# The opening of a mixture-of-experts layer: routing from unnormed residuals, one turn to tokens, and a gather that holds the tokens

## The reference, cut to what matters

```python
h2 = rms_norm(x, norm2_g[l]) * (1.0 + scale2) + shift2
x = x + gate2 * expert_choice_ffn(h2, w_router[l], b_router[l], w_gate[l], w_up[l], w_down[l])

def expert_choice_ffn(h, w_router, b_router, w_gate, w_up, w_down):
    cap = (EC_CAPACITY_FACTOR * S) // N_EXPERTS            # 2 * 512 / 16 = 64 places per expert
    affinity = jax.nn.softmax(h @ w_router + b_router, axis=-1)
    gates, idx = lax.top_k(affinity.transpose(0, 2, 1), cap)
    xin = h[bidx, idx]                                      # 16 experts x 64 tokens x 1024
    hid = silu(xin @ w_gate) * (xin @ w_up)                 # 1024 -> 2048
    y = hid @ w_down * gates[..., None]                     # 2048 -> 1024
    return zeros_like(h).at[bidx, idx].add(y)
```

## Time and profile before

| | us |
|---|---|
| median of 3 runs | 2590.87 (2590.12 to 2594.27) |
| the profiled execution: its time | 2594.25 |
| the profiled execution: its span | 2592.4 |
| PE busy | 2382.4 (92%) |
| DVE, ACT busy | 1006.2 (39%), 620.6 (24%) |
| read from HBM | 590.37 MB |

### The profile page before, as it was taken

How to read it: one execution, slowest core, us unless ns; L and a number is a source line. 1 busy time by engine, 2 the same in 40 slices (tenths; PEclk the granted TensorE clock), 3 DMA queues, 4 the chain that set the end, 5 groups by cost and what they waited for, 6 DMA issues and landing times.

```text
span 2592.4 us, 23747 instructions
## 1 busy us (share of the span) xinstructions
PE 2382.4 (92%) x9961; PEld 1394.2 (54%) x9961; DVE 1006.2 (39%) x1616; ACT 620.6 (24%) x1002; POOL 112.4 (4%) x120
## 2 busy tenths in 40 slices
PE   5999988899999999999789979799898989989888
PEld 2445544588888788888667737333232323233222
DVE  4555463366663666564556372301111011101011
ACT  2112163333223333233446464110000000000000
POOL 2000000000000000000221312000000000000000
PEclk8999988999999999999899999899999999999999
DMA  9312330355553145550211203599999999999997
GB/s 352 105 65 81 109 118 0 114 182 190 174 184 128 49 163 195 195 179 33 89 49 33 94 29 130 215 427 429 431 430 432 430 431 431 431 430 432 429 431 316
DMA packets 121024, 594.04 MB, mean 229 GB/s; under 512 B 9346, under 2 KB 10880, under 8 KB 95318
## 3 DMA queue, kind: packets, MB, share of 16 engines
q1 hardware_dynamic: 117522, 583.23, 56.7%
q0 software_dynamic: 3088, 9.17, 1.0%
q10 hardware_dynamic: 308, 0.13, 0.0%
HBM read 590.37 MB, written 2.13 MB: 229 GB/s over the span
## 4 chain that ended last, share of the span: by engine, by line
PE 77%; DMA 12%; DVE 6%; ACT 3%; issue 1%; POOL 0%; DVEq 0%; ACTq 0%; POOLq 0%
PE PS L1150 15%; PE PS L840 9%; PE PS L842 9%; PE PS L841 9%; PE PS L656 8%; PE PS L891 5%; PE PS L149 5%; PE PS L1167 3%; DMA RING<-in_w_down_dram 3%; PE PS L1177 2%; PE PS L564 2%; DMA RING<-in_w_gate_dram 2%; PE PS L740 2%; DMA RB_a<-in_w_down_dram 2%; DMA RING<-in_w_up_dram 2%; PE PS L591 1%
## 5 line engine op out<-in xcount | busy, mean ns | idle before, releaser
L1150 PE MATMUL PS<-RING,HID_e 128*64 128x512 f32 x608 | 204.9, 607 | 9.1 <-DMA RING<-in_w_up_dram 4.7
L1150 PE MATMUL PS<-RB_a,HID_e 128*64 128x512 f32 x576 | 195.6, 598 | 5.2 <-DMA RB_a<-in_w_up_dram 4.5
L1150 PE MATMUL PS<-AT_g,HID_e 128*64 128x512 f32 x288 | 130.6, 601 | 5.1 <-DMA AT_g<-in_w_up_dram 4.2
L1150 PE MATMUL PS<-HID_e 128*64 128x512 f32 x288 | 130.8, 602 | 4.5 <-DMA HID_e<-in_w_gate_dram 2.7
L1150 PE MATMUL PS<-XT,HID_e 128*64 128x512 f32 x288 | 130.8, 602 | 4.3 <-DMA XT<-in_w_gate_dram 2.7
L2476 DVE TENSOR_TENSOR TMP<-TMP,PS 128x512 f32<-128x512 f32 x32 | 19.8, 683 | 284.6 <-PE PS L1150 284.6
L1167 PE MATMUL PS<-RING,HID_e 128*64 128x512 f32 x288 | 112.1, 656 | 13.0 <-DMA RING<-in_w_down_dram 13.0
L1696 ACT ACTIVATE PADS<-PS 128x512 f32<-128x512 f32 x8 | 4.8, 597 | 490.3 <-PE PS L149 490.3
L2484 DVE TENSOR_TENSOR HID_e<-PS,HID_e 128x512 f32<-128x512 f32 x16 | 10.3, 686 | 278.3 <-PE PS L1167 278.3
L1167 PE MATMUL PS<-RB_a,HID_e 128*64 128x512 f32 x304 | 107.3, 624 | 11.0 <-DMA RB_a<-in_w_down_dram 11.0
L1150 PEld LDWEIGHTS PS<-RING,HID_e 128*64 128x64 f32 x608 | 61.7, 139 | 97.7 <-issue 84.5
(11 more groups left out here) (448 smaller groups left out, 4712.9 us busy)
## 6 DMA issues: line engine op xcount, KB each, us to landing
RING<-in_w_gate_dram SPq DMA_DIRECT2D x19, 2048.0 KB, 22.0
RING<-in_w_up_dram SPq DMA_DIRECT2D x19, 2048.0 KB, 18.3
RB_a<-in_w_down_dram SPq DMA_DIRECT2D x19, 2048.0 KB, 21.6
RB_a<-in_w_gate_dram SPq DMA_DIRECT2D x18, 2048.0 KB, 22.4
RB_a<-in_w_up_dram SPq DMA_DIRECT2D x18, 2048.0 KB, 17.6
RING<-in_w_down_dram SPq DMA_DIRECT2D x18, 2048.0 KB, 21.9
RING<-in_mlp_w_dram SPq DMA_DIRECT2D x32, 1024.0 KB, 5.8
RB_a<-in_mlp_w_dram SPq DMA_DIRECT2D x32, 1024.0 KB, 5.3
```

What stands on the lines that cost most here:

```text
L1150: last = pe.matmul(b[64 * d:64 * d + 64, :], xv_[:, k, 64 * d:64 * d + 64], wv, start=k == 0, stop=k == 7)
```

## The change

What is computed stays the same in exact arithmetic. The norm of a token is a factor 1/r of its row, so it is taken out of every product and put in at the end:

- **Router by tokens.** `wr` is multiplied once by the norm's gain (`g2s2`) and the shift's share of the logits is added to the bias (`router_b`); both happen in the mLSTM stage, with a chain of eight matmuls on PE and two operations on DVE. The router's products go into four banks of 128 tokens x 16, XT held and `wr` moving, four feature tiles in the middle of part 6 and four after it; DVE multiplies by 1/r and adds the bias. The norm is no longer spread (L612), multiplied (L1816) or written to AT4 (L1290).
- **Softmax** on 128 x 64 at once; an empty exponential ahead of it has the table loaded.
- **Tokens turned once.** XT is turned, 32 transposes; ACT writes each bank twice, to `h2t` and to `acc`.
- **Gather.** `Pm` carries 1/r. `h2t` is held (every eighth column), `Pm` moves (128 columns), so the result has features on partitions; DVE and ACT write it to `xins` with gain and shift, four tiles each. Its copies to `xtok` and the transposes back go.
- **Gain and shift** in the order of every eighth feature come from a small round trip through HBM on SP (`gvec`), in the mLSTM stage.
- **Slots.** The slot in HID3 is filled first, the one in AT4 needs only the end of part 6, XT's comes last and needs only the turns. The scratch rows `af, wk0, wk1, pos` move to another place. PADS is zeroed ahead of BD.

```diff
@@ sync_program @@
+                if b == 1:
+                    w.wait_ge(*V_ml.at("g"))
+                    for i, v in enumerate((g2s2, mod2[:, 24:32])):
+                        sp.dma_start(gvec[i].rearrange("(k p) -> p k", p=128), v,
+                                     allow_slow_non_contiguous=True).then_inc(*D["gp"].up("out", i))
+                elif b == 2:
+                    w.wait_ge(*D["gp"].at("out", 1))
...
-            big.freed[4] = ((S_moe, "h2", 3, 1), (T_moe, "router"))
-            big.freed[5] = ((S_moe, "acc", 3, 1),)
-            big.freed[6] = ((T_moe, "pos"),)
+            big.freed[0] = ((T_dil, "pv", 3), (V_dil, "logit", 15, 1))
+            big.freed[1] = (*ring.freed[0], *ring.freed[1])
+            big.freed[2] = (*ring.freed[2], *ring.freed[3])
+            big.freed[3] = big.freed[4] = big.freed[5] = ((T_out, "out2", 1, 3),)
+            big.freed[6] = ((T_moe, "tok", 3, 1), (S_nrm, "sq", 7, 7))
@@ pe_mlstm @@
+            b = banks.take(w, ("const",), (V_moe, "const"))
...
+            chain(pe, b[:, 0:16], [(mod2[:, 24 + k:25 + k].to_broadcast([128, 128]), wr[:, k, :]) for k in range(8)]).then_inc(
+                *T_moe.up("const"))
             bs = pe_open(pe, w, 1, lambda j: ((S_ml, "so", j),))
@@ pe_dilated @@
-            pe_parts(pe, w, 6, bs, range(8), AL3, AH3, out2_fed)
+            pe_parts(pe, w, 6, bs, range(4), AL3, AH3, out2_fed)
+            rbs = [banks.take(w, ("router", i), (V_moe, "logits", i)) for i in range(4)]
+            pe_router(pe, w, rbs, range(4))
+            pe_parts(pe, w, 6, bs, range(4, 8), AL3, AH3, out2_fed)
+            pe_router(pe, w, rbs, range(4, 8))
+        def pe_router(pe, w, bs, ks):
...
+            for k in ks:
+                w.wait_ge(*V_out.at("out2", k, 0))
+                for i, b in enumerate(bs):
+                    last = pe.matmul(b[:, 0:16], XT[:, k, i * 128:(i + 1) * 128], wr[:, k, :], start=k == 0, stop=k == 7)
+        def pe_gather(pe, w, n, hf):
...
+            w.wait_ge(*V_moe.at("P", n, 3, 1, 0))
+            w.wait_ge(*S_moe.at("h2", 3, 1))
+            for k in range(4):
+                last = chain(pe, b[:, 128 * k:128 * k + 128],
+                             [(h2t[:, i, 4 * hf + k::8], Pm[n % 2][:, i, :]) for i in range(4)])
@@ pe_experts @@
+            pe_norm_cols(pe, w, 7, 512, (S_nrm, "root", 7))
+            for i in range(2):
+                pe_to_tokens(pe, w, i, 0)
+                pe_to_tokens(pe, w, i, 1)
             b = banks.take(w, ("affT",), (V_moe, "affT"))
...
             for hf in range(2):
                 b = banks.take(w, ("g2b", hf), (S_moe, "g2b", hf))
+                w.wait_ge(*V_moe.at("top", 5))
...
             for hf in range(2):
-                pe_gather_rows(pe, w, 0, hf)
+                pe_gather(pe, w, 0, hf)
             pe_gate_turn(pe, w, 0)
-            for hf in range(2):
-                pe_gather_turn(pe, w, 0, hf)
@@ act_experts @@
             act_norm_root(act, w, 7, lambda k: XT[:, k, :], 512, lambda k: V_out.at("out2", k, 0))
+            act.activation(rm[:, 0:1], rm[:, 0:1], ACT.Exp, bias=0.0, scale=0.0).then_inc(*S_moe.up("table"))
+            act_to_tokens(act, w, 0, 0)
             w.wait_ge(*V_moe.at("neg"))
+            act.activation(ST[:, 0:64], loose[:, 0:64], ACT.Exp, bias=0.0, scale=1.0).then_inc(*S_moe.up("soft"))
@@ dve, mLSTM stage @@
+            dve.memset(PADS[:, :, :], 0.0).then_inc(*V_ml.up("pad_zero"))
             w.wait_ge(*D["blk"].all())
...
-            dve.memset(PADS[:, :, :], 0.0).then_inc(*V_ml.up("pad_zero"))
+            w.wait_ge(*T_moe.at("const"))
+            w.wait_ge(*D["br"].all())
+            dve.tensor_tensor(router_b, banks.of("const")[:, 0:16], router_b, ALU.add).then_inc(*V_moe.up("const"))
+            dve.tensor_tensor(wr[:, :, :], wr[:, :, :], g2s2.rearrange("p (k o) -> p k o", o=1).to_broadcast([128, 8, 16]),
+                              ALU.mult).then_inc(*V_moe.up("wr"))
@@ dve_chosen, dve_experts @@
+                    dve.tensor_scalar(Pm[x][:, i, cs], iota64, posc[:, i, e:e + 1], norm_col(7, 4 + i), ALU.is_equal,
+                                      ALU.mult).then_inc(*V_moe.up("P", n, i, d, 0))
...
+            dve.memset(af, 1.0).then_inc(*V_moe.up("af"))
+            w.wait_ge(*S_nrm.at("root", 7))
...
+                dve.scalar_tensor_tensor(out=lgs[:, i, :], in0=banks.of("router", i)[:, 0:16], scalar=norm_col(7, 4 + i),
+                                         in1=router_b, op0=ALU.mult, op1=ALU.add).then_inc(*V_moe.up("logits", i))
+            w.wait_ge(*S_moe.at("table"))
...
-            dve.memset(af, 1.0).then_inc(*V_moe.up("af"))
```

More of the change, by code:

```diff
@@ L1105, in pe_gather_rows, with pe_to_tokens @@
+        def pe_to_tokens(pe, w, i, hf):
+            b = banks.take(w, ("tok", i, hf), (S_moe, "acc", i, hf))
+            w.wait_ge(*V_out.at("out2", 7, 0))
+            transposes(pe, b, [XT[:, 4 * hf + k, i * 128:(i + 1) * 128] for k in range(4)]).then_inc(*T_moe.up("tok", i, hf))
+        def pe_gather(pe, w, n, hf):
+            b = banks.seat(w, 4 + hf, ("x", n, hf), (S_moe if hf else V_moe, "x", n, 4 * hf + 3))
+            w.wait_ge(*V_moe.at("P", n, 3, 1, 0))
             w.wait_ge(*S_moe.at("h2", 3, 1))
-            chain(pe, b, [(Pm[n % 2][:, i, :], h2t[:, i, hf * 512:(hf + 1) * 512]) for i in range(4)]).then_inc(
-                *T_moe.up("x", n, hf))
+            for k in range(4):
+                last = chain(pe, b[:, 128 * k:128 * k + 128],
+                             [(h2t[:, i, 4 * hf + k::8], Pm[n % 2][:, i, :]) for i in range(4)])
+            last.then_inc(*T_moe.up("x", n, hf))
@@ L1112, in pe_gate_turn @@
             transposes(pe, b, [Pg[n % 2][:, i, :] for i in range(4)]).then_inc(*T_moe.up("pt", n))
[L1114 to L1118, removed]
         def pe_between(pe, w, n, k):
@@ L1145, in pe_up @@
                 for k in range(8):
+                    w.wait_ge(*(S_moe if k > 3 else V_moe).at("x", n, k))
                     for c, b in enumerate(bs):
@@ L1180, in pe_experts @@
         def pe_experts(pe, w):
-            pe_norm(pe, w, 7, 512)
-            for i in range(3):
-                pe_to_tokens(pe, w, "acc", XT, i, V_out.at("out2", 7, 0))
-            b = banks.take(w, ("router",), (S_moe, "router"))
-            for k in range(8):
-                w.wait_ge(*D["wr"].all())
-                w.wait_ge(*S_nrm.at("out", 7, k))
-                last = pe.matmul(b[0:16, :], wr[:, k, :], AT4[:, k, :], start=k == 0, stop=k == 7)
-            last.then_inc(*T_moe.up("router"))
-            b = banks.take(w, ("lg",), (S_moe, "soft", 3))
-            w.wait_ge(*S_moe.at("router"))
-            for i in range(4):
-                last = pe.transpose(b[:, 16 * i:16 * i + 16], wk1[:, i * 128:(i + 1) * 128], ident[0:16, 0:16])
-            last.then_inc(*T_moe.up("lg"))
+            pe_norm_cols(pe, w, 7, 512, (S_nrm, "root", 7))
+            for i in range(2):
+                pe_to_tokens(pe, w, i, 0)
+                pe_to_tokens(pe, w, i, 1)
             b = banks.take(w, ("affT",), (V_moe, "affT"))
@@ L2399, in dve_chosen @@
             x = n % 2
+            for i in range(4):
+                for d in range(2):
+                    e, cs = 2 * n + d, slice(64 * d, 64 * d + 64)
+                    dve.tensor_scalar(Pm[x][:, i, cs], iota64, posc[:, i, e:e + 1], norm_col(7, 4 + i), ALU.is_equal,
+                                      ALU.mult).then_inc(*V_moe.up("P", n, i, d, 0))
             if n >= 2:
```

131 lines of the change are left out of this document (55 added, 76 removed).

## The result

The changed kernel is slower by 0.8%. Its median is **2613.93 us** (2610.81 to 2616.09, 4 runs) against 2592.55 us for the kernel before (2590.12 to 2594.27, 4 runs), a ratio of 1.0084 with a 95% interval of 1.0068 to 1.0100. The forecast was 2580.4 us.

A forecast was written before the change was run, and what follows sets the result against it. The prediction took the weight stream, begun by the first gate matmul, to bound the kernel. Opening 12.3 us, less 1.4 upstream and 0.35 first pair, saved 10.5 us: profiled 2583.7, median 2580.4 us, range 2575.5 to 2587.

The forecast's parts named there:

- The end moves one for one with the start of the first gate matmul: Weight stream: cannot be shortened, only begun earlier, so the kernel's end shifts exactly as the first gate matmul does.
- Inside the stream about 10.2 us of PE work per pair may be added before anything moves.: Expert pairs: DMA busy all 117 us, PE 106.75 us, so about 10.2 us more PE work is free.
- I take 0.136: Gather: 0.136 us per full-clock record, from strided transposes; opening's gather 10.5 us, 1.3 us dearer than before.
- Rival B: Gather in all pairs: strided hold makes PE the bound above 0.29 us a record; 2618.5 us at 0.35; chance 0.05.
- rival A: Opening: light matmuls leave the clock low, router's second half 7.5 us, gather 15.0 us; total 2589.2 us; chance 0.13.
- 3.2 us are added outright: Router's first half inside part 6: 32 records of 0.1 us on dense PE, costing 3.2 us.
- gain 12.9: From part 6's end to the first top-k round: norm, router, softmax and turn shortened, 12.9 us saved.
- rival C: Opening: clock never falls, so sums, affinity turn and gather are cheaper; total 2576 us; chance 0.12.
- Memset and one-hot matrices, 1.9: Top-k to gather: memset moved into a DVE wait gains 0.5 us, fewer one-hot operations ahead of the gather 1.4.
- after the gather, 2.0: Between gather's end and first gate matmul: only four transposes, 0.6 us, are left; 2.0 us saved.
- upstream 1.4: mLSTM stage: DVE's new wait for PE's chain of eight matmuls delays the convolution taps, costing 1.4 us.
- First pair, 0.35: First expert pair: next gathers ahead of the fourth-quarter release, 8.7 us for 8.35, widen the DMA gap; costs 0.35 us.

The follow-up runs named there:

- experiment 7: Changed kernel with each pair's gather replaced by another form (transposes, 512 or 64 moving columns, strided or contiguous operands); one execution, 2631.6 us.
- experiments 4 and 5: 4: changed kernel, both gather halves behind the last gate tile, 2613.15 us; 5: changed kernel with contiguous hold, gather lengthened differently per pair, 2605.0 us.
- experiment 6: Changed kernel with another step of the gather's held operand in each pair (1 to 16, one with operands swapped); one execution, 2598.7 us.
- experiment 3: Changed kernel, but DVE adds the first four residual tiles before it sums their squares; 2607.79 us, ratio 1.0052.
- experiment 1: Changed kernel, but ACT writes h2t in gather order, so the held 128 columns are contiguous; 2590.93 us, ratio 0.9993.
- experiment 2: Changed kernel, but all 64 router records stand behind part 6, strided hold kept; 2605.82 us, ratio 1.0055.

## Why the prediction was wrong, step by step

- **"The end moves one for one with the start of the first gate matmul"** held for the kernels with a contiguous hold, and not for the changed one: its start moved by 2 us and its end by 21. Failed by the step below.
- **"Inside the stream about 10.2 us of PE work per pair may be added before anything moves."** This step failed. It stands for some 12 of the 18.9 us that are lost behind the first gate matmul; the first pair, below, has the other 7. The gather added 7.3 us of PE work, less than the 10.2, and each pair became 2.2 us longer. PE's room per pair is a sum over 117 us; the loads need releases at their time. The block ahead of the fourth release, not the sum, had to be held against the loads in hand. Rows of before could have told it: the earlier trace rows give the block, the rhythm of the issues. The earlier trace rows also show 22.8 us for a load to land, 4.7 loads in hand. I had weighed releases against transfers for "the DMA gap of 0.5 us there grows to 0.85", and did it for the first pair only.
- **Gather, "I take 0.136".** This term was mis-sized, and it is what set off the step above. A record took 0.243 in the opening and 0.244 in the stream: 15.54 us for 10.5, so 5.0 us in the opening, and 15.6 us for the 8.7 that a pair was to have. The price came from strided transposes, and experiment 7 shows that transposes don't pay it. Rival B named the mechanism, with its place; its threshold of 0.29 us a record was too high (loads come late from about 13.3 / 64 = 0.21, by experiments 4 and 5), so I gave it 0.05 and a price (27 us in seven pairs) for a record of 0.35 that never came. What B expected as its sign, PE's busy time near 117 us, didn't show (110.95), and the time was lost nonetheless. That the opening's gather came near rival A's 15.0 us is chance: the granted clock was back at 1.00 from about 1646, and the records stayed at 0.24.
- **The Trainium skill's rule that I weighed.** At step 8 a record cost double, 0.244 for 0.118 us. The Trainium skill ("SBUF — State Buffer", section "Door 1: The DMA port swizzle", the note on cachelines) says that at least two hits in a 16-byte line are needed for full bandwidth, and that float32 may be strided by four for free. The first half agrees with experiment 6: two hits a line (step 2) are nearly free, one hit (step 4 and up) costs the full price, and step 3 lies between. The second half does not: step 4 took 0.240 us. The measurement decides. I had let the transposes' row overrule a rule that spoke against the change.
- **Router, first half: "3.2 us are added outright".** Part 6 grew by 13.3. Three terms were missing. PE paused 3.48 us for DVE's fourth residual tile, since the router's fourth bank is free only when DVE has read that tile from it; the block on ACT's squares ahead of it stood in before's timeline, and I had not put the new wait against it. The light records, "0.1 us each" by the one-column row, took 0.218 after that pause and 0.135 without it (experiment 3). And the dense records behind them paid 2.8 us for the clock.
- **Part 6 to the first top-k round: "gain 12.9".** Measured 14.1. Right, and the 1.2 on top are rival C's term: the router's second half and the norm's sums ran at a granted clock of 1.00 (1613.5 to 1617), the sums took 0.90 us for 1.62 and the affinities' turn 0.61 for 1.04. Rival A's clock fall came, but ahead of this stretch, inside part 6, where I had not looked for it.
- **Memset and one-hot matrices, 1.9; after the gather, 2.0; upstream 1.4.** Measured 2.1, 2.2 and 1.2, of which 0.7 reached part 6. Right. ACT's later copies and the two round trips of the gain vectors were hidden, as said; the table's load stood on the chain with its 1.28 us, as the sum had it.
- **First pair, 0.35.** It was 7.1: 111.0 us from its first gate matmul to the next pair's, against 103.9 before and 104.0 in experiment 1. The count was the right one, the gather's size was not.

The two faults account for the miss but for some 3 us: without the strided hold and with the router behind part 6 the kernel takes 2583.7 us against the forecast's 2580.4, with the router spread 2581.5.

## What to carry to other kernels

When a stream of loads goes through few slots, don't ask how much room an engine has over a period; count the loads in hand at each release, and hold them against the longest piece of work in front of the next release. Price an operand's stride by a row of the same operation and width: here transposes hid it, wide moving tiles hid it, and narrow matmuls doubled. Before small matmuls are pushed into a dense phase, look at what their input's writer has in its own list, and place them in small lots or behind the phase.

## What the runs showed of the hardware that I had not expected

- The price of a stride saturates: 0.125 us a record at step 2, 0.181 at 3, and 0.224 to 0.244 from 4 to 16, for the held and the moving operand alike.
- It doesn't depend on TensorE's clock. In the opening of the changed kernel a strided record took 0.24 us at a granted clock of 0.50 (16 records in the 4 us from 1640) and 0.244 in the stream at 1.00. So the stride nearly doubles a record's price only at full clock, where the contiguous one takes 0.118; at 0.50 the contiguous one takes about 0.21 itself (an estimate from experiment 1's opening gather: 9.62 us for 64 records, some 4.7 us of it at a granted clock of 0.50, the rest at 0.118 a record).
- The clock fell to its lower level while PE was busy without idle time, under records with 16 moving columns; they ran at 0.11 us at first, in experiment 2. Lots of eight between dense groups didn't bring it down.
- A fallen clock isn't back when dense work resumes: after the router's first half 48 dense records took 13.74 us for 10.9, and the granted clock was 0.50 until about 1605, 5 us into them.
